# One 128-token tile at a time through attention, mix and routing in two of the four half-passes of a two-layer decoder step

## The reference, cut to what matters

```python
xn = rms_norm(x, norm1_g)
z, xbc, dt_raw, q, k, v, iq, ik, iw, gate_a, gate_b = split(xn @ w_in)
y_a = mamba2_branch(...)                 # chunks of 128 tokens, state carried on
y_b = dsa_prompt(...)                    # block of 128 queries, keys up to them
x = x + (sigmoid(gate_a) * (y_a @ w_branch_a) + sigmoid(gate_b) * (y_b @ w_branch_b)) @ w_out
x = x + peer_ffn(rms_norm(x, norm2_g), peer_wq, peer_keys, peer_u, peer_v)

def one(xb):                             # in peer_ffn, one block of tokens
    s = einsum(xb @ wq, keys)            # 8 heads x 2 halves x 128 keys
    ...                                  # 16 best of each half, 16 best pairs: eidx, g
    act = gelu(einsum('thkd,td->thk', u[eidx], xb))
    return einsum('thk,thkd->td', g * act, v[eidx])
```

## Time and profile before

| | before |
|---|---|
| median of 3 runs | 5604.73 us (5594.49 to 5608.93) |
| span of the profiled execution, its own time here | 5599.6 us |
| mean granted TensorE clock | 0.870 of full |
| busy PE / DVE / ACT / POOL | 77% / 63% / 22% / 44% |
| DMA | 1484.67 MB, mean 265 GB/s |
| layer 0: first half up to its routing / second half | 0 to 1072 / 1072 to 2336 us |
| layer 1: first half / second half | 2362 to 3659 / 3659 to 4924 us |
| stage `last` | 4924 to 5600 us |

### The profile page before, as it was taken

How to read it: one execution, slowest core, us unless ns; L and a number is a source line. 1 busy time by engine, 2 the same in 40 slices (tenths; PEclk the granted TensorE clock), 3 DMA queues, 4 the chain that set the end, 5 groups by cost and what they waited for, 6 DMA issues and landing times. The chain is left out here.

```text
span 5599.6 us, 50197 instructions
## 1 busy us (share of the span) xinstructions
PE 4306.3 (77%) x15868; PEld 2641.6 (47%) x15868; DVE 3537.3 (63%) x7830; ACT 1216.0 (22%) x3039; POOL 2480.1 (44%) x2215
## 2 busy tenths in 40 slices
PE   7956886578577988689677676968678798767777
PEld 6334775543333765263334565554344476223333
DVE  4055638866677546686666848966667754854544
ACT  2042311121332112120422311121242211111111
POOL 0000010166555544546565332456555554477776
PEclk9975997689789999799898888988889899888888
DMA  4311631389787987889889966688888798799999
GB/s 141 118 60 41 229 124 61 118 294 349 269 272 267 334 284 272 278 308 371 290 292 323 339 203 199 203 286 323 306 274 274 264 359 281 249 361 409 409 409 361
DMA packets 579390, 1484.67 MB, mean 265 GB/s; under 512 B 60104, under 2 KB 251176, under 8 KB 572616
## 3 DMA queue, kind: packets, MB, share of 16 engines
q0 software_dynamic: 307200, 1115.82, 55.2%
q1 hardware_dynamic: 258968, 331.39, 17.8%
q10 hardware_dynamic: 12960, 34.26, 1.6%
HBM read 1435.37 MB, written 45.93 MB: 265 GB/s over the span
## 5 line engine op out<-in xcount | busy, mean ns | idle before, releaser
L2721 PE MATMUL duo<-vring,diag 128*128 128x512 f32 (+1 forms) x2976 | 1509.2, 657 | 401.1 <-DMA vring<-in_peer_v,eidx 173.2
L2593 POOL DMA_INDIRECT uring<-in_peer_u,eidx x981 | 1140.5, 1163 | 1112.3 <-DVE uring L2629 658.0
L2674 POOL DMA_INDIRECT vring<-in_peer_v,eidx x1024 | 1134.0, 1107 | 1067.0 <-PE duo L2721 472.7
L2721 PEld LDWEIGHTS duo<-vring,diag 128*128 128x128 f32 (+1 forms) x2976 | 589.6, 208 | 1197.3 <-issue 944.6
L2629 DVE SCALAR_TENSOR_TENSOR uring<-uring,xr 128x1024 f32<-128x1024 f32 x795 | 958.9, 1221 | 204.6 <-DMA uring<-in_peer_u,eidx 178.8
L689 PE MATMUL duo<-wx,xT 128*128 128x512 f32 (+3 forms) x1440 | 605.1, 578 | 32.9 <-PEq L133 32.1
L2754 DVE SCALAR_TENSOR_TENSOR x_tok<-vring,wt,x_tok 128x1024 f32<-128x1024 f32 x296 | 385.0, 1301 | 97.0 <-DMA vring<-in_peer_v,eidx 70.4
L2702 ACT ACTIVATE diag<-ident,wt 128x128 f32<-128x128 f32 x728 | 269.8, 395 | 748.4 <-PE duo L2721 678.8
L689 PEld LDWEIGHTS duo<-wx,xT 128*128 128x128 f32 (+1 forms) x1440 | 238.9, 176 | 385.8 <-issue 383.1
L2629 DVE SCALAR_TENSOR_TENSOR uring<-uring,duo 128x1024 f32<-128x1024 f32 x201 | 245.4, 1221 | 264.4 <-DMA uring<-in_peer_u,eidx 263.9
L533 PE MATMUL duo<-xT,wx 128*128 128x264 f32 (+1 forms) x1536 | 357.6, 397 | 36.5 <-ACT newcols L556 30.6
(11 more groups left out here) (472 smaller groups left out, 5283.8 us busy)
## 6 DMA issues: line engine op xcount, KB each, us to landing
wx<-in_w_in SPq DMA_DIRECT2D x32, 2048.0 KB
wx<-in_w_in SPq DMA_DIRECT2D x48, 1024.0 KB, 8.3
wm<-in_w_in SPq DMA_DIRECT2D x32, 1024.0 KB, 10.4
wm<-in_w_branch_a SPq DMA_DIRECT2D x32, 1024.0 KB, 11.6
wq<-in_peer_wq SPq DMA_DIRECT2D x32, 1024.0 KB, 8.7
tokm<-tout ACTq DMA_DIRECT2D x64, 256.0 KB
eb<-decays SPq DMA_DIRECT2D x32, 512.0 KB, 4.5
s_h<-in_state_ssm SPq DMA_DIRECT2D x16, 1024.0 KB, 8.3
```

Of the source, the lines that this page charges most:

```text
L2593: pool.indirect_dma_start(out=E.rings.urows[K % E.ur], out_offset=None, in_=table, in_offset=bass.IndirectOffsetOnAxis(ap=E.tiles[q][3][:, ...
L2674: pool.indirect_dma_start(out=E.rings.vrows[K % E.vr], out_offset=None, in_=table, in_offset=bass.IndirectOffsetOnAxis(ap=E.tiles[q][3][:, ...
L2721: mm = pe.matmul(G.bank[6 + c][0:m, :], G.diag[:, R % DR, 0:m], E.rings.vrows[K % E.vr][:, c * BANK:(c + 1) * BANK], start=first, stop=las ...
```

## The change

Two of the four half-passes, layer 0's first and layer 1's last (`SPLIT`), no longer run attention, mix, norm2, scores and routing for both tiles together. They run them for the first tile (stages with the suffix `_a`), then for the second (`_b`); the last half takes the sample tokens along in `_b`. `Back` holds the tiles of such a part and its first column in the activations. `start_experts` is now called after `route_a` in a split half, so that the job of that half is open beside the `_b` stages: up to 120 dots (`SPLIT_AT`) by the end of `route_b`. In layer 0 the sums of these experts run beside `_b` as well (88 by the plan's weights); in layer 1 the sums of the half before are still running there, and all sums of the last half stay in `last`. The sampling of layer 0 begins after tile 1's attention, as before, and now runs beside the `_b` stages. In the last half the slots are ordered tile 2, sample, tile 3. The extra `peer_u` buffer of the last job goes. All weights of the plan are new, scaled to what is left in each stage.

```diff
 UR, VR, DR = 5, 4, 4
-UR2, VR2 = 1, 14
+VR2 = 14
...
+    def backs(self, split):
+
+        if not split:
+            return [Back(self, (0, 1), "", self.late)]
+        return [Back(self, (0,), "_a", False), Back(self, (1,), "_b", self.late)]
+
+
+class Back(Half):
+
+
+    def __init__(self, half, js, suffix, sample):
+        self.i, self.js, self.suffix, self.late, self.split = half.i, js, suffix, sample, len(js) < 2
+        self.tiles = tuple(half.tiles[j] for j in js)
+        self.c0 = js[0] * P
+        self.last = js[-1] == 1
+        self.n_out = len(js) * P + (DECB if sample else 0)
+
+    def key(self, name):
+        return name + self.suffix
...
-        sg = Region(nc, f"x{l}_", G.region)("sg", [P, 2, 2, n]) if H.late else sb("sg", [P, 2, 2, n])
+        sg = Region(nc, f"x{l}_", G.region)("sg", [P, 2, 2, n]) if H.late and not H.split else sb("sg", [P, 2, 2, n])
-        acts = {"ga": G.xT, "a": G.yaT, "gb": G.xT, "b": G.ybT}
+        acts = {"ga": (G.xT, H.c0), "a": (G.yaT, H.c0), "gb": (G.xT, H.c0), "b": (G.ybT, 0)}
+                        act, c0 = acts[name]
-                            mm = pe.matmul(tile_bank(c, part, f)[:, 0:n], w[u % NW][:, k, f * P:(f + 1) * P], acts[name][:, k0 + k, 0:n],
+                            mm = pe.matmul(tile_bank(c, part, f)[:, 0:n], w[u % NW][:, k, f * P:(f + 1) * P], act[:, k0 + k, c0:c0 + n],
...
-                for j in range(2):
+                for j in range(nt):
-                    mm = pe.matmul(G.bank[2][:, 2 * P:n], kT[:, f % 2], q[:, f % 2, 2 * P:n], start=True, stop=True)
+                    mm = pe.matmul(G.bank[2][:, nt * P:n], kT[:, f % 2], q[:, f % 2, nt * P:n], start=True, stop=True)
...
+        if split_at is not None and H.late:
+            self.tiles = [self.tiles[1], self.tiles[0], self.tiles[2]]
...
+        elif q == 1 and E.split_at is not None:
+            yield float(E.split_at)
...
+        state.earlier, state.xr0, state.E = (0, 0, 0, 0, 0), [0, 0], None
+
+        def start_experts(H, l, split):
+            last = H.late and l == DEPTH - 1
+            if last:
+                nu = UR
+                rings = Rings([G.uring[:, r, :] for r in range(UR)], [G.vring[:, r, :] for r in range(VR)],
+                              G.sample_sems[0:nu], G.sample_sems[nu:nu + VR + VR2], False)
+            else:
+                rings = Rings([G.uring[:, r, :] for r in range(UR)], [G.vring[:, r, :] for r in range(VR)], G.rowu, G.rowv, True)
+            order, dots, sums = PLANS[(l, H.i)]
+            E = Experts(G, l, H, state.earlier, list(state.xr0), rings, GROUP_LAST if last else GROUP, SPLIT_AT if split else None)
+            for q in range(len(E.tiles)):
+                state.xr0[q % 2] += 1
+            E.assign(spans(E, order, dots, sums), SHARES)
+            state.earlier = E.later()
+            if last:
+                E.copy_rows(SPLIT_AT if split else dots["route2"], G.sample_sems[len(rings.usems) + len(rings.vsems)])
+            G.beside.begin("U", Job(DOTS, E, E.dots_end, dots, order))
+            state.E, state.sums = E, Job(SUMS, E, E.sums_end, sums, order)
+
+        def choose(H, K, l):
+
+            G.g2src = G.norm2_g[l]
+            last = H.late and l == DEPTH - 1
+            with ExitStack() as peer:
+                score = peer.enter_context(ExitStack())
+                wq, pk = (score.enter_context(nc.sbuf_tensor(name, shape, F32, side="right", allow_name_mangling=True))
+                          for name, shape in (("wq", [P, 3, KD, 2 * P]), ("pk", [P, 3, 2, P])))
+                norm_tokens(nc, G, K, KD, K.key("norm2"), K.late,
+                            [[(wq[:, u], query_weights(G, l, u)), (pk[:, u], key_rows(G, l, u))] for u in range(2)], rows_out=G.xn2)
+                S = Names()
+                S.ps = sb("ps", [P, len(K.tiles), 2 * PH, NK], stack=peer)
+                if K.late:
+                    S.pss, S.psl = sb("pss", [P, 2, DECB, PH], stack=peer), sb("psl", [DECB * PH, 2, NK], stack=peer)
+                    S.es, S.gs = sb("esmp", [DECB * PH, 1, PK], I32, stack=peer), sb("gsmp", [DECB * PH, 1, PK], stack=peer)
+                peer_scores(nc, G, S, K, l, wq, pk, K.key("pscore"))
+                score.close()
+                turns = peer.enter_context(ExitStack())
+                vectors = ()
+                if K.late and not last:
+                    rows, taps = (turns.enter_context(nc.sbuf_tensor(name, shape, F32, side="right", allow_name_mangling=True))
+                                  for name, shape in (("gain_rows", [32, P]), ("tap_rows", [BC_ROWS, CD])))
+                    vectors = vector_loads(G, l + 1, rows, taps)
+                peer_routes(nc, G, S, K, l, 0, vectors, K.key("route"))
+                if not K.split:
+                    G.beside.finish("U")
+                    if not H.late:
+                        G.beside.finish("V")
+                    start_experts(H, l, False)
+                    if H.late:
+                        peer_routes(nc, G, S, K, l, 1, (), "route2")
+                        G.beside.finish("V")
+                    G.beside.begin("V", state.sums)
+                    if H.late and not last:
+                        turn_vectors(nc, G, l + 1, rows, taps, False)
+                elif not K.last:
+                    if state.E is not None:
+                        G.beside.finish("U")
+                    earlier_sums = state.E is not None
+                    start_experts(H, l, True)
+                    if not earlier_sums:
+                        G.beside.begin("V", state.sums)
+                elif H.late:
+                    G.beside.finish("V")
+                    G.beside.begin("V", state.sums)
+
         for l in range(DEPTH):
             for H in (Half(0), Half(1)):
...
+                    backs = H.backs((l, H.i) in SPLIT)
+                    for K in backs:
+                        with ExitStack() as mixing:
+                            G.ybT, wm = (mixing.enter_context(nc.sbuf_tensor(name, [P, KD, cols], F32, side="right", allow_name_mangling=True))
+                                         for name, cols in (("ybT", K.n_out), ("wm0", 2 * P)))
+                            for j, t in zip(K.js, K.tiles):
+                                rows = slice(t * P, (t + 1) * P)
+                                attention_inputs(nc, G, A, l, P, t, t * P, j == 0,
+                                                 (G.k_prompt[l, 0, rows].rearrange("t h d -> t (h d)"),
+                                                  G.v_prompt[l, 0, rows].rearrange("t h d -> t (h d)"), G.idx_k_prompt[l, 0, rows]), K.key("qkv"))
+                                attention_prompt(nc, G, A, l, t, j - K.js[0], j == 0, [(wm[:], gate_weights(G, l))] if j == K.js[-1] else [],
+                                                 K.key(f"attn{j}"))
+                            if K.last and not H.late:
+                                order = tuple(K.key(name) for name in ORDER_SAMPLE[:4]) + ORDER_SAMPLE[4:]
+                                plan = PLAN_SAMPLE_SPLIT if K.split else PLAN_SAMPLE
+                                G.beside.begin("S", Job(SAMPLE, Sample(nc, G, l, G.region), SAMPLE_TIME, plan, order))
+                            G.mixT = mixing.enter_context(nc.sbuf_tensor("mixT", [P, KD, K.n_out], F32, side="right", allow_name_mangling=True))
+                            mix_branches(nc, G, K, l, wm, K.key("mix"))
+                        if not K.last:
+                            choose(H, K, l)
+                choose(H, backs[-1], l)
+        state.E.rings.vrows += [more[:, r, :] for r in range(VR2)]
...
-ORDER_FIRST = ("norm1", "xbc", "tokproj", "ssd", "ssmout", "ssd", "ssmout", "qkv", "attn0", "qkv", "attn1", "mix", "norm2", "pscore", "route")
-ORDER = (("route2", "vectors") + ORDER_FIRST, ORDER_FIRST[:3] + ("convst",) + ORDER_FIRST[3:] + ("route2",))
-ORDER_SAMPLE = ("mix", "norm2", "pscore", "route", "norm1", "xbc", "tokproj")
+SPLIT = ((0, 0), (1, 1))
+SPLIT_AT = 120
+FRONT = ("norm1", "xbc", "tokproj")
+SCANS = ("ssd", "ssmout", "ssd", "ssmout")
+BACK = ("mix", "norm2", "pscore", "route")
+BACK_A = ("qkv_a", "attn0_a", "mix_a", "norm2_a", "pscore_a", "route_a")
+BACK_B = ("qkv_b", "attn1_b", "mix_b", "norm2_b", "pscore_b", "route_b")
+ORDER_LATE = FRONT + ("convst",) + SCANS + ("qkv", "attn0", "qkv", "attn1") + BACK + ("route2",)
+ORDER_NEXT = ("route2", "vectors") + FRONT + SCANS + ("qkv", "attn0", "qkv", "attn1") + BACK
+ORDER_SAMPLE = BACK + FRONT
-PLAN_DOTS = ({"route2": 22, "vectors": 4, "norm1": 0, "xbc": 37, "tokproj": 90, "ssd": 10, "ssmout": 3, "attn0": 14, "attn1": 26, "mix": 54,
-              "last": 247, "last_rush": 0.88},
-             {"norm1": 0, "xbc": 50, "tokproj": 85, "convst": 5, "ssd": 10, "ssmout": 2, "attn0": 22, "attn1": 24, "mix": 51})
-PLAN_SUMS = ({"vectors": 8.5, "tokproj": 12, "ssd": 18, "ssmout": 7, "qkv": 9, "attn0": 18, "attn1": 30, "norm2": 5, "mix": 34,
```

(58 more changed lines are left out.)

65 lines of the change are left out of this document (5 added, 60 removed).

## The result

The changed kernel takes 5865.55 us (median of 4 runs, 5863.41 to 5873.91) against 5599.61 beside it (5581.27 to 5608.93): a ratio of 1.0488, 95% interval 1.0463 to 1.0513, 266 us slower. The profiled execution spans 5864.7 us.

What follows compares the result with a forecast made beforehand. It saw an underused head, a middle bound by several things with DMA near its limit, and a DMA-bound tail. Layer 0's +113 and layer 1's +102 gave +215 us on the span: 5820 us, 8-in-10 range 5640 to 5905.

Steps and rivals of the forecast that it cites:

- Two DMA prices: Whole kernel: a gather in the tail costs 1.338 us of DMA time, weights cost 3.01 us per MB.
- Layer 1: Second half +205, early stages +28 and tail -131 sum to +102 us.
- Layer 0, tile 0's pass: Layer 0's first half: tile 0's mix, norm, scores and routing now stand alone, adding 205 us.
- Layer 0, second half: Layer 0's second half gives back 207 gathers, 0.63 us each, for -131 us.
- tile 1's mix in layer 0: Layer 0's first half: tile 1's mix beside sampling and gathers takes 315 us (283 to 376), +35 on 280.4.
- I take 225 to 230: Tile 1's mix in layer 0 without experts, in us, between 198 (TensorE sets the pace) and 280 (sampling's chain does).
- 100 gathers at 0.96: Gathers beside tile 1's mix in layer 0, priced in us each from layer 1's mix, bring it to about 322.
- tile 1's pass: Layer 0's first half: attention, mix, norm, scores and routing of tile 1 beside sampling and experts, +39 us.
- B: Rival, both layers: gaps absorb doubled weights and gathers, -61 us, 5540; needs the queues' share above 78.4%; chance 0.14.
- +50: Layer 1's total in us if its stages reach full DMA share and the early part is free too.
- C: Rival: layer 0's head absorbs (tile 1's mix 283, second half returns 190), layer 1 does not; 5730 us, chance 0.17.
- D: Rival, split mixes and scores: TensorE becomes the bound through weight loads or a lower clock; 5970 us, chance 0.12.

Runs made afterwards that it cites:

- e5: Changed kernel with all four split mixes loading half of each weight unit and using it twice; +185 us against the kernel before on its chip.
- e3: Changed kernel, both splits kept, but layer 0's first experts start only after tile 1's routing; 5837.38 us, ratio 1.0442 to the kernel before.

## Why the prediction was right, and where it was off

**Two DMA prices.** The gather's was right: the tail shortened by 132 us (forecast 131), at 1.346 us a gather. The weights' 3.01 us per MB held as occupancy: q1 has 20.7% of the new span for 401.65 MB, 3.02 us per MB. Taken out of a stage bound by DMA, a MB returned less, 2.4 to 2.6 us (e5).

**Layer 1.** +105 in the spans, +108 when split alone, for +102. Mix a 155, mix b 164, scores a 64, scores b 75: 458 us for 459 forecast. That the sum is exact is partly luck: the working gives the mixes 310 and the scores 150 us, and they took 319 and 139. Two of the eight `wq` loads of a scores stage are issued in the norm stage before it, so the scores had less to load than the 28.4 us entered; their DMA share rose to 0.98 in b, above the 0.96 taken as the most, and was 0.81 in a. Attention with its inputs, at 275 against 263, cost 12 where 3 were forecast; most of that is a `qkv` of tile 3 of 30 us instead of 22. Norm came to 38 for 34, routing to 174 for 179.

**Layer 0, tile 0's pass.** 196 for 205: mix 92 (95), norm 13 (11), scores 38 (43), routing 54 (56).

**Layer 0, second half.** -133 for -131: token projection -30 (-26), scans -34 (-28), attention -26 (-30), mix -18 (-19), norm and xbc -14 (-20), norm, scores and routing -8 (-8), and `convst` -2.

**The term that was mis-sized** is tile 1's mix in layer 0: +35 forecast, +81 measured, 46 of the 50 us between forecast and result. Its working had two steps. "I take 225 to 230" without experts was 258: I let the stage shed most of its 82 us of matmuls because TensorE had been busy for 239 of 280. When the matmuls went, TensorE's idle time, nearly all of it before the sampling's matmuls, grew by 43 us, and what was left ran at a clock of 0.80 for 0.92 (e3). Then "100 gathers at 0.96" was 103 us, near the 96 of that price. The working itself led to 322, and taking 315 gave 7 more away. The rest of tile 1's pass came to 12 us over the forecast: the scores (+3 for +6), the routing (-4 for -14), norm (+5 for +2) and attention (+13 for +10). Tile 0's pass and the second half gave 11 back.

**The rivals.** B fails at its own threshold: 75.3% against 78.4. (Its layer 0 adds up to +32, not +26, and "+50" for layer 1 with the early part free should be +46; neither moves the forecast.) C's head didn't absorb: 361, not 283, and the second half gave 133 back, not 190. D's weight loads didn't show. TensorE's timeline in the changed kernel, in tile 0's mix:

```profile
499.88 3.84 PE L2212 MATMUL duo<-ybT,wm 128*128 128x128 f32 x32
```

(3.84 - 0.28) / 31 = 0.115 us a matmul, close to the 0.11 of the forecast. The clock's part of D was seen, 0.77 in tile 1's mix beside sampling, and its share of the 30 us missed there isn't separated. In layer 1's mixes, at 0.85 and 0.89, e5 shows DMA as the bound; its mix a then ran at 0.94.
